# Two crowded experts of a 32-expert loop are moved from loop places 13 and 19 to 11 and 21

## The chip, the cores and the metric
The program runs on one core of one Trainium2 chip. The metric is the time of one execution on the device in microseconds (us); the median of several runs is quoted. "The profiled execution" is one further run whose every instruction was recorded.

## The reference
A sequence of 256 tokens with 1024 features passes through two transformer-like blocks in float32. The first block is a gated recurrence with stick-breaking attention and a convolutional feed-forward part. The second has two kinds of attention and ends in a mixture of experts, which is the part that matters here:

```python
logits = (xf @ w_router + b_router)              # 256 tokens, 32 experts
top_val, top_idx = lax.top_k(logits, 4)          # each token goes to 4 experts
gates = jax.nn.softmax(top_val, axis=-1)
# for every expert e, with the tokens that chose it:
hid = xb @ w_mlp1[e] + b_mlp1[e]                 # 1024 -> 2048
glu = jnp.minimum(hid[..., ::2], 7.0)
lin = jnp.clip(hid[..., 1::2], -7.0, 7.0)
act = glu * jax.nn.sigmoid(1.702 * glu) * (lin + 1.0)
y = act @ w_mlp2[e] + b_mlp2[e]                  # 1024 -> 1024
# out[token] = sum over its experts of gate * y
```

The 256 tokens make 1024 assignments, 32 an expert on average. Every expert's weights, 8 MB and 4 MB, are read from the device's memory once. The order in which the experts are worked through does not change what is computed, apart from rounding.

## The kernel before
The first 740 us or so compute everything up to the router. Then a loop over 32 places begins, one expert at a place. All weights pass through a ring of 17 slots in on-chip memory (`RING = 17`), each slot of 1 MB. An expert takes 12 pieces: 8 of the first matrix ("up") and 4 of the second ("down"). The pieces are loaded and used in a fixed order: up(0), then for each x up(x+1) and down(x). So the first piece of up(x) is number 12x - 4 (`up_at`, line 395), and the last one of all is number 383.

The order of loads is the SyncE queue's (`sync_program`, lines 456 to 466). For piece i it waits until piece i - 17 has been used, and only then issues the load:

```python
e.wait_ge(S.m_piece, i - RING + 1)        # TensorE has used piece i - 17
second, value = K.second_use(i - RING)
e.wait_ge(second, value)                  # line 460: ... and used it a second time, if the expert is crowded
```

A loop place handles a block of up to 64 tokens (`CAP = 64`). On TensorE it is: `up_bias` and 64 matmuls of `up` (line 961), the gather of the next expert's tokens (888), the four down pieces of the expert before (994), transposes (899, 904, 894), and on every second x, `add_pair` (1032), which adds two experts' results to the output. An expert with more than 64 tokens is "crowded": a second block of tokens goes through the same weights while they are still in the ring. `second_block` gathers it, `second_up` (983) does 64 more matmuls, `second_down` (the same line 994, and 1013) 32 more and the sum. Its slots come free only after that second use.

Which expert stands at which place is decided while the kernel runs. `ranks` on VectorE (line 2123) gives each expert a key, its token count times 32 plus a tie value, and its rank is the number of experts with a larger key. Experts 0 and 1 have a large tie value, so they have ranks 0 and 1 and stand at places 0 and 1 always, since their loads start before the routing is known. For the others the host prepares `at`, the rank that is wanted at each place (line 2407), from the list `PLACES`: the most crowded expert goes to the first place of the list, the next to the second, and so on.

```python
at = np.argsort(PLACES)                   # line 2407, host
ts_(K.sel96, at, K.rk[:, 1:2], None, ALU.is_equal)   # ranks(): place of each expert
```

All instructions are in the order in which the program's text puts them on each engine; nothing is reordered by a planner. The list `PLACES` is a constant at the top of the file, so no function's text changes. A program prints what it can find of the functions here:

Of the kernel before, what the change touches and what calls it, by code (L numbers as in the profile page):

```python
# [23 lines left out]
SCN = 14344  # L24


PLACES = [13, 19, 7, 25, 16, 10, 22, 4, 28]
PLACES = [0, 1] + PLACES + [n for n in range(2, NE) if n not in PLACES]


# [2318 lines left out]
def lay_out(i):  # L2349
# [56 lines left out]
    tie = np.where(e < 2, 2.0 ** (20 - e), 1.0 * e)  # L2406
    at = np.argsort(PLACES)
    o["rankc"] = np.concatenate([rep, np.ones((96, 1)) * tie, np.ones((96, 1)) * at], 1).astype(np.float32)
# [21 lines left out]
```

## Time and profile before

| | |
|---|---|
| median of 3 runs | 1726.02 us (1725.83 to 1738.32) |
| profiled execution | 1724.05 us, span of its instructions 1722.3 us |
| TensorE matmuls | 1612.9 us busy, 94% of the span |
| TensorE weight loads | 896.4 us |
| VectorE | 584.1 us |
| ScalarE | 350.6 us |
| bytes moved | 545.47 MB, mean 317 GB/s |

The span runs from the first to the last recorded instruction. Busy shares are averages over parts of the program with different limits, and a matmul that runs counts as busy whether or not the memory would have been the limit at that point; so the loop has to be read stretch by stretch. All times in the rows below are microseconds from the start of the span unless they are marked ns.

### The profile page before, as it was taken

Reading aid. Unit: us, or ns where it says so; the run is one execution under the profiler, and the core shown is the slowest. Engines: PE = TensorE matmul, PEld = TensorE weight load, DVE = VectorE, ACT = ScalarE, POOL = GpSimd, SP = SyncE. Lnnn points to the kernel's source line nnn. Section 1 sums busy time; section 2 is a strip of 40 time slices with the busy share of each in tenths; the row PEclk is TensorE's granted clock in tenths of the full one; section 3 lists DMA queues with packets and bytes.
Section 4 is the critical chain, followed back from the end, with each engine's and each line's share of the span. In section 5 each row is a group of like instructions: output and inputs, shape, how many; then the busy total and the mean of one; then the engine's idle time right before and its main releaser. Section 6 shows DMA issues by size and latency. Waiting matters only on the chain. (4 is left out here: it accounts for less than half of the span.)

```text
span 1722.3 us, 20673 instructions
## 1 busy us (share of the span) xinstructions
PE 1612.9 (94%) x7402; PEld 896.4 (52%) x7402; DVE 584.1 (34%) x1338; ACT 350.6 (20%) x651; POOL 0.2 (0%) x4
## 2 busy tenths in 40 slices
PE   5999989899999898889999998899999999999997
PEld 3888878788888776633333322233333333333222
DVE  2547762789710454331221111111112112211112
ACT  2125562332200134120111101101111011111111
POOL 0000000000000000000000000000000000000000
PEclk9999999999999988988999999999999999999999
DMA  9936665458963330248999999999999999999995
GB/s 397 385 125 254 244 269 184 160 200 325 389 243 125 123 122 1 98 156 357 420 420 419 421 420 421 420 420 421 418 421 385 364 387 420 420 421 420 420 420 235
DMA packets 77220, 545.47 MB, mean 317 GB/s; under 512 B 8944, under 2 KB 9456, under 8 KB 11536
## 3 DMA queue, kind: packets, MB, share of 16 engines
q1 hardware_dynamic: 76048, 542.31, 78.0%
q8 instruction: 93, 1.52, 0.4%
q10 hardware_dynamic: 1024, 1.18, 0.2%
q14 instruction: 55, 0.45, 0.1%
HBM read 542.41 MB, written 1.05 MB: 316 GB/s over the span
## 5 line engine op out<-in xcount | busy, mean ns | idle before, releaser
L961 PE MATMUL bank<-ring,scr 128*64 128x512 f32 x2048 | 456.0, 598 | 18.3 <-DMA ring<-in_w_mlp 18.3
L510 PE MATMUL bank<-hT,ring 128*128 128x256 f32 x1728 | 384.9, 384 | 10.3 <-ACT hT L1141 7.2
L510 PEld LDWEIGHTS bank<-hT,ring 128*128 128x128 f32 x1728 | 332.5, 193 | 60.7 <-issue 15.1
L961 PEld LDWEIGHTS bank<-ring,scr 128*64 128x64 f32 x2048 | 143.2, 138 | 313.5 <-issue 256.6
L994 PE MATMUL bank<-ring,hT 128*64 128x512 f32 x1024 | 233.9, 597 | 2.5 <-DMA ring<-in_w_mlp 2.5
L2215 DVE TENSOR_SCALAR scr<-bank 128x256 f32<-128x256 f32 x64 | 27.0, 421 | 395.5 <-PE bank L961 395.5
L994 PEld LDWEIGHTS bank<-ring,hT 128*64 128x64 f32 x1024 | 68.4, 136 | 141.3 <-issue 130.5
L2285 DVE COPY hT<-bank 64x512 f32<-64x512 f32 x32 | 22.2, 695 | 315.4 <-PE bank L994 285.9
L1452 ACT ACTIVATE scr<-scr 128x256 f32<-128x256 f32 x64 | 26.7, 417 | 503.2 <-DVE scr L2215 503.2
L1569 DVE SCALAR_TENSOR_TENSOR ring<-ring,cb 128x1024 f32<-128x1024 f32 x80 | 94.5, 1219 | 0.0
L674 PE MATMUL bank<-scr,ring 128*128 128x256 f32 x384 | 83.5, 379 | 1.6 <-ACT scr L1295 1.6
L674 PEld LDWEIGHTS bank<-scr,ring 128*128 128x128 f32 x384 | 72.9, 190 | 11.9 <-ACT scr L1295 2.0
L888 PE MATMUL bank<-scr 128*64 128x512 f32 x272 | 69.9, 639 | 7.2 <-DVE scr L2185 4.6
L1486 ACT ACTIVATE hT<-bank 128x512 f32<-128x512 f32 x32 | 19.1, 598 | 221.7 <-PE bank L904 221.7
L1032 PE MATMUL bank<-hT,scr 128*128 128x512 f32 x128 | 59.2, 605 | 0.8 <-ACT hT L1502 0.8
L888 PEld LDWEIGHTS bank<-scr 128*64 128x64 f32 x272 | 20.0, 146 | 47.8 <-issue 39.3
L1032 PEld LDWEIGHTS bank<-hT,scr 128*128 128x128 f32 x128 | 23.0, 189 | 37.6 <-issue 35.9
L904 PEld LDWEIGHTS bank<-con,scr 128*128 128x128 f32 x136 | 14.9, 146 | 35.2 <-issue 26.7
L2173 DVE COPY scr<-bank 64x256 f32<-64x256 f32 x64 | 27.1, 423 | 13.1 <-PE bank L894 11.8
L1634 DVE RECIPROCAL scr<-scr 128x512 f32<-128x512 f32 x8 | 26.8, 3352 | 10.3 <-ACT scr L1172 10.3
L1888 DVE SCALAR_TENSOR_TENSOR scr<-scr,col 128x256 f32<-128x256 f32 x48 | 23.1, 481 | 20.4 <-ACT scr L1295 20.1
L1928 DVE SCALAR_TENSOR_TENSOR xT<-bank,modc,xT 128x256 f32<-128x256 f32 x8 | 3.5, 479 | 77.4 <-PE bank L674 77.4
(389 smaller groups left out, 1350.2 us busy)
## 6 DMA issues: line engine op xcount, KB each, us to landing
ring<-in_w_mlp SPq DMA_DIRECT2D x384, 1024.0 KB, 23.1
ring<-in_w_in SPq DMA_DIRECT2D x28, 1024.0 KB, 24.4
ring<-in_up SPq DMA_DIRECT2D x24, 1024.0 KB, 6.8
ring<-in_w_ada SPq DMA_DIRECT2D x24, 1024.0 KB, 7.0
ring<-in_ada_w SPq DMA_DIRECT2D x16, 1024.0 KB, 5.0
ring<-in_down SPq DMA_DIRECT2D x12, 1024.0 KB, 15.4
ring<-in_ada SPq DMA_DIRECT2D x8, 1024.0 KB, 14.8
ring<-in_w2in SPq DMA_DIRECT2D x6, 1024.0 KB, 9.7
```

The source lines that it names most:

```text
L510: ins = mm(b[:, 256 * j:256 * j + 256], v[:, k * 256 + j * 128:k * 256 + j * 128 + 128], rhs[:, k, :], start=(k == 0), stop=(k == 7))
L674: ins = mm(b[j][:, 0:256], v[:, k * 256 + j * 128:k * 256 + j * 128 + 128], K.ff[:, kk * 8 + k, :], start=(kk == 0 and k == 0), stop=(kk = ...
L888: ins = mm(B[3][64 * hf:64 * hf + 64, :], K.sel[c][:, tt, :], K.h4[:, tt, hf * 512:(hf + 1) * 512], start=(tt == 0), stop=(tt == 1), skip_ ...
L961: ins = mm(HID[0][n][64 * hf:64 * hf + 64, :], K.xe[0][x % 2][:, xo:xo + 64], v[:, o0:o0 + 512], start=False, stop=(k == 7), skip_group_ch ...
L994: ins = mm((K.down_bank(x), B[1])[c][g:g + 64, :], K.aT[c][x % 2][:, 128 * q + 64 * hf:128 * q + 64 * hf + 64], v[:, j * 1024 + oh * 512:j ...
L1032: ins = mm(OUT[tt][oh][:, :], K.pairT[p % 2][oh][:, tt * 128:(tt + 1) * 128], K.ypair[oh], start=False, stop=False, skip_group_check=True)
L1452: act(K.w2[:, sl], K.actb[0][:, sl], ACT.Sigmoid, scale=1.702).then_inc(S.m_sig, 1)
L1569: ins = stt(w, w, 1.0, K.cb[:, :], ALU.mult, ALU.mult, accum_out=K.modc[:, n // 3, m:m + 1])
L1634: e.reciprocal(rst, rst).then_inc(S.vec, done.one())
L1888: stt(w[:, m, :], u[:, m, 1:257], C("fw", 48 + n), w[:, m, :], ALU.mult, ALU.add).then_inc(S.vec, done.one())
L2173: ins = e.tensor_copy(K.pairT[x // 2 % 2][g ^ x % 2][rows, :], B[3][rows, 0:256])
L2215: ts_(w[:, sl], gate, 7.0, None, ALU.min).then_inc(S.m_glu, 1)
```

## The change
The list of wanted places is another one. Places 0 and 1, the completion of the list by the places that it leaves out, and everything else are as before.

```diff
-PLACES = [13, 19, 7, 25, 16, 10, 22, 4, 28]
+PLACES = [11, 21, 27, 6, 16, 8, 24, 13, 18]
 PLACES = [0, 1] + PLACES + [n for n in range(2, NE) if n not in PLACES]
```

The most crowded expert among 2 to 31 moves from place 13 to 11, the next from 19 to 21, the third from 7 to 27, the fourth from 25 to 6, and so on. The number of instructions in the program's text does not change.

## Rows read from the trace of the kernel before

**Rows 1.** The page, 40 slices of 43 us: rate of all transfers.

```profile
GB/s 397 385 125 254 244 269 184 160 200 325 389 243 125 123 122 1 98 156 357 420 420 419 421 420 421 420 420 421 418 421 385 364 387 420 420 421 420 420 420 235
```

**Rows 2.** Windows: length, busy of PE, PEld, DVE, ACT, POOL; clock, DMA share, GB/s.

```profile
1050.00:1100.00 50.00, 44.92 (x198) 13.79 (x196) 7.88 (x22) 4.21 (x9) 0.00 (x0) 1.00 1.01 420
1320.00:1420.00 100.00, 95.94 (x434) 32.92 (x432) 16.81 (x46) 9.56 (x19) 0.00 (x0) 0.98 0.91 367
1430.00:1500.00 70.00, 70.00 (x330) 24.25 (x328) 13.87 (x38) 8.24 (x17) 0.00 (x0) 1.00 1.01 420
```

**Rows 3.** TensorE's timeline, starts of up groups: start, length, [idle before <- releaser].

```profile
1085.88 8.75 PE L961 MATMUL bank<-ring,scr 128*64 128x512 f32 x40
...
1133.79 13.90 PE L983 MATMUL bank<-ring,scr 128*64 128x512 f32 x64
...
1230.07 13.90 PE L961 MATMUL bank<-ring,scr 128*64 128x512 f32 x64
...
1254.48 13.90 PE L961 MATMUL bank<-ring,scr 128*64 128x512 f32 x64
...
1282.68 13.90 PE L961 MATMUL bank<-ring,scr 128*64 128x512 f32 x64
...
1329.52 13.90 PE L983 MATMUL bank<-ring,scr 128*64 128x512 f32 x64
...
1425.41 13.90 PE L961 MATMUL bank<-ring,scr 128*64 128x512 f32 x64
```

**Rows 4.** Groups of instructions: line, shapes, count, busy us, mean ns, idle before.

```profile
L983 PE MATMUL bank<-ring,scr 128*64 128x512 f32 x128 | 27.8, 592 | 0.0
```

**Rows 5.** TensorE's timeline, four pieces that were used as they landed.

```profile
979.19 1.94 PE L961 MATMUL bank<-ring,scr 128*64 128x512 f32 x8 [0.47 <-DMA ring<-in_w_mlp]
...
1099.87 1.94 PE L961 MATMUL bank<-ring,scr 128*64 128x512 f32 x8 [0.55 <-DMA ring<-in_w_mlp]
...
1615.21 1.94 PE L961 MATMUL bank<-ring,scr 128*64 128x512 f32 x8 [0.53 <-DMA ring<-in_w_mlp]
...
1703.44 1.94 PE L994 MATMUL bank<-ring,hT 128*64 128x512 f32 x8 [0.52 <-DMA ring<-in_w_mlp]
```

**Rows 6.** Line 462, one load each (pieces 140, 188): issue, then landing.

```profile
L462 SPq DMA_DIRECT2D ring<-in_w_mlp x1: 5789/5789/5789, 1052.6 to 1052.6; - x1
DMA to landing us min/median/max: 29.5/29.5/29.5
...
L462 SPq DMA_DIRECT2D ring<-in_w_mlp x1: 333/333/333, 1182.0 to 1182.0; - x1
DMA to landing us min/median/max: 20.3/20.3/20.3
```

**Rows 7.** The same for pieces 240 and 272.

```profile
L462 SPq DMA_DIRECT2D ring<-in_w_mlp x1: 1632/1632/1632, 1306.5 to 1306.5; - x1
DMA to landing us min/median/max: 26.8/26.8/26.8
...
L462 SPq DMA_DIRECT2D ring<-in_w_mlp x1: 337/337/337, 1411.3 to 1411.3; - x1
DMA to landing us min/median/max: 13.5/13.5/13.5
```

**Rows 8.** Line 462, loads issued between 1142 and 1210 us.

```profile
DMA to landing us min/median/max: 11.2/15.3/24.6
```

**Rows 9.** Line 462, loads issued between 1306.5 and 1411.6 us.

```profile
DMA to landing us min/median/max: 4.6/8.7/26.8
```

**Rows 10.** SyncE's waits, 1300 to 1430 us: total, times, longest.

```profile
SPq L460 <- PE bank L983: 31.0, 8, 23.3
```

**Rows 11.** The chain of waits that ended last: start, length, link.

```profile
1677.00 26.39 DMA ring<-in_w_mlp
```

## The prediction
> **What bounds the kernel now.** I read the rate of transfers first, over the whole span [rows 1]. In the expert loop, from about 775 us on, it stands at 420 GB/s in almost every slice: the loop is bound by the loading of the weights. Three slices fall below, 385, 364 and 387, between 1292 and 1421 us; there something else was the limit. The windows confirm both: 420 GB/s in 1050 to 1100 us, where TensorE is busy 44.92 of 50 us and so has time to spare, 367 in 1320 to 1420 us, 420 again from 1430 us [rows 2].
>
> What happened in between is seen on TensorE and in SyncE's queue. The second block's matmuls, 128 in all, are exactly two groups of 64, at 1133.79 and 1329.52 us [rows 3, 4]. So two experts are crowded, and they stand at places 13 and 19, as the list says. Around the second one SyncE waits up to 23.3 us for that line before it may issue the next load [rows 10], and the loads of that stretch land 4.6 us after issue at the least [rows 9]: the queue had run dry and each load found idle transfer engines. Around the first crowded expert the fastest landing took 11.2 us [rows 8]: loads still queued, and no slice falls. At the end the last link of the chain is a load again, and the last piece is used as it lands [rows 5, 11]. Hence a transfer time lost anywhere in the loop stands whole in the end, and what follows the last landing (1703.4 to 1722.3 us, 18.9 us) is not touched.
>
> **The pace of both sides.** Landings: piece 99 is used at 979.19 us (the last of up(8)) and piece 147 at 1099.87 us (the last of up(12)), both as they landed: 120.68 / 48 = 2.514 us a piece, 30.17 us an expert of 12. From piece 348 to 383, at the end, it is 88.23 / 35 = 2.521 us [rows 5]. TensorE, when it never waits: up(16) to up(17) 24.41 us, up(17) to up(18) 28.20 us (with the pair's sum), 52.61 us for two, 26.3 us an expert [rows 3]. So TensorE makes up 60.34 - 52.61 = 7.73 us in two experts. A crowded expert costs it: up(18) to up(22) took 142.73 us in place of 105.22, that is 37.5 us more, or 9.7 experts' worth of catching up [rows 3].
>
> **How far TensorE is behind.** I take as lag the start of up(x) less the landing of its first piece. At up(12) it is 1085.88 - (1052.6 + 29.5) = 3.8 us. At up(16), past the first crowded expert, 1230.07 - (1182.0 + 20.3) = 27.8 us [rows 3, 6]. By up(18) it has come down by 7.7 to 20.1 us, and there the second one begins, with 16.3 us more lag than the first had. The ring covers the first one's case and not this.
>
> **The loss, by three counts.** Piece 240 landed at 1306.5 + 26.8 = 1333.3 us, piece 272 at 1411.3 + 13.5 = 1424.8 us [rows 7]: 91.5 us for 32 pieces, 80.4 at 2.514, so **11.1 us** lost. From piece 147 to 348 it is 515.34 us for 201 pieces; at 2.514 they take 505.3, at 2.521 506.7: 10.0 or 8.6 lost [rows 5]. By the rate, (1 - 367/420) of 100 us is 12.6 us [rows 2]. I take 11, because its two landings lie closest around the stall, and keep 8.6 and 12.6 as ends. Since 16.3 us of additional lag cost 11, some 5.3 us of it were still covered.
>
> **The change, part by part.** Nothing is removed or added: as many matmuls, loads, waits and branches, the same work on VectorE in the ranking, with another constant. What moves is this.
>
> (a) The first crowded expert, from 13 to 11. Its additional work begins at the end of place 10. TensorE has caught up with the landings in up(8), at 979 us [rows 5], so it meets place 11 as it met place 13, pinned to the landings; 11 is odd as 13 is, so the pair's sum falls the same way. Its cost to the transfers is that of before, nothing: the cover is the ring, 11.2 us of queue at the narrowest [rows 8]. If that were gone, the cost would be the idle transfer time, at most the 11 us seen at place 19. The lag at up(14) is then the 27.8 us that up(16) had.
>
> (b) The second, from 19 to 21. From up(14) to up(20) are three pairs: 27.8 - 3 x 7.73 = 4.6 us. Within up(20) TensorE takes 13.90 / 8 = 1.74 us a piece against 2.51, so it waits for the eighth if the lag at its start is below 7 x 0.78 = 5.4 us. It is: TensorE is pinned again, as at up(12) with 3.8. And were it 4.6 in full, it is 0.8 above 3.8, under the 5.3 that is covered. The loss of 11 us goes.
>
> (c) The end. Lag at up(24) 27.8 us, at up(30) 4.6, so at up(31) it has caught up. From up(31) to the use of piece 383, 15 landings take 37.7 us, TensorE's work 13.9 + 7 x 1.74 + 3.8 (the pair) = 29.9; another 7.8 us of lag would not show at all.
>
> (d) The uncrowded experts, third rank and below, change places. None has a second block [rows 4], each has the same 12 loads and the same matmuls. An unseen cost is that of other addresses in another order; from both sides, the difference between the two measured paces, 0.007 us x 383 = 2.7 us, more or less. I take none, for both paces were measured across many different experts.
>
> **The sum.** 1724.05 - 11 = 1713.0 us for the profiled execution. It stands 1.97 us under the median of 1726.02, so the median becomes **1715.0 us**, 0.64% less. 1% is 17.3 us, about what a measurement of this kernel can tell from no change.
>
> **A rule that speaks against it.** Spacing matters only because loading leaves TensorE little to catch up with. To work off 37.5 us in six experts it needs 6.25 an expert, so loads that take 26.3 + 6.25 = 32.6 us an expert or more, 12.58 MB in 32.6 us or 387 GB/s and less. Below that rate six places apart are as good as ten, and the time stays at 1726 us. The rows show 420 GB/s in both calm windows [rows 2]. The Trainium skill, "DMA: Bandwidth & Descriptors", section "Specifications", gives about 358 GB/s as the limit of memory for one core, which is below that point; its section "Bandwidth" says that both cores of a pair must be streaming for it. The trace does not agree with the plain limit, by 62 GB/s, so the case gets 1 of 100.
>
> **The rivals.**
> - *Only the place of the stall moves* (6%). The second crowded expert still finds too much lag at up(20), or the first at 11, and part of the transfers' idle time remains. Each us of lag beyond 3.8 + 5.3 = 9.1 at up(20) costs one. If TensorE made up 5 us a pair in place of 7.7, the lag were 12.8 and 3.7 us of the 11 stayed: 1719. Against it stands 52.61 us for two, on the trace without a wait.
> - *Nothing comes of it* (4%, with the 1% of the slower rate). Loading is not what the end waits for: 1726. Against it, the last piece used as it landed [rows 5].
> - *A late end, slower than before* (3%). After place 21 only ten experts are left to catch up in. If TensorE made up d us an expert, the end came 27.8 - 7d - 7.8 us late against the landings. From d = 1.3 down that is more than the 11 won; at d = 0 (15% slower an expert, as if the granted clock fell at times after the second crowded expert) it is 20 - 11 = 9 us slower, 1735. The trace has d = 3.86, and the clock at 1.00 from 1430 to 1500 us [rows 2]; nothing speaks for it.
> - *The change does not do what it says*: the crowded ones aren't ranks 2 and 3, or land at other places. The groups at places 13 and 19 exclude the first [rows 3]; 1%, at 1726.
>
> **How the numbers follow.** The forecast has 86%. Its own range is 1726 less 12.6 and less 8.6, 1713.4 to 1717.4, plus the 2.7 us of (d) either way: 1710.7 to 1720.1. That holds also the first rival's usual case; what is left out (no effect, late end, a small part for surprises) is some 15%. Faster by over 1% (below 1708.8) needs half as much again as was lost: 4%. Slower by over 1% (above 1743.3): 2%; the late end as priced doesn't reach it. Within 1%: 94%.
>
> **What would show it.** Right: no slice of the loop below 415 GB/s until the last; the second-block groups near 1133.8 - 60.3 = 1073.5 and, ten experts of 30.17 us later, 1375 us; landings after both no faster than about 11 us; up(20) with short waits for loads; the last piece about 1692.4 us. The steps fail one by one: (a) if the rate falls near 1130 us, (b) if it falls near 1400 us, (c) if the last pieces are used long after landing, (d) if the pace in calm stretches isn't 2.51 us a piece. The whole would be wrong if the rate is level throughout and the time still stays.

## The result and the profile after

| | before | after |
|---|---|---|
| median | 1726.02 us (20 runs) | 1715.91 us (20 runs) |
| profiled execution, span | 1722.3 us | 1713.9 us |
| ratio of times | | 0.9936, 95% interval 0.9919 to 0.9953 |

The forecast was 1715.0 us, in a range of 1710.7 to 1720.1. The kernel became faster by 0.64%. That is less than the 1% which the prediction took as what a measurement can tell from no change, but the interval of the ratio lies clear of one.

The page of the changed kernel, its line of the rate in 40 slices of 42.8 us, stands against [rows 1]:

```profile
GB/s 397 389 115 264 247 270 185 161 201 320 364 255 124 125 146 1 99 106 359 420 420 420 420 420 420 421 415 421 419 420 420 420 420 407 421 420 420 420 421 219
```

The three slices of 385, 364 and 387 are gone. Two shallow ones came, 415 and 407. They stand behind the two crowded experts at their new places; a repeat of this kernel, further down, shows only the second. The windows answer to [rows 2]; the columns are the same:

```profile
1050.00:1100.00 50.00, 42.98 (x188) 15.08 (x187) 9.62 (x28) 5.73 (x11) 0.00 (x0) 0.93 1.01 420
1320.00:1420.00 100.00, 92.15 (x417) 31.30 (x417) 17.60 (x50) 10.52 (x20) 0.00 (x0) 0.97 1.01 420
1430.00:1500.00 70.00, 69.30 (x326) 24.12 (x324) 12.69 (x35) 8.38 (x16) 0.00 (x0) 1.00 1.01 412
```

From 1320 to 1420 us the rate rose from 367 to 420. What is left of a loss, 412 in the last window, is 70 x 8/420 = 1.3 us.

TensorE's timeline, beside [rows 3], shows where the second blocks stand now (line 983) and up(20) ahead of the second of them:

```profile
1060.64 13.90 PE L961 MATMUL bank<-ring,scr 128*64 128x512 f32 x64
1074.81 13.90 PE L983 MATMUL bank<-ring,scr 128*64 128x512 f32 x64
...
1330.16 12.18 PE L961 MATMUL bank<-ring,scr 128*64 128x512 f32 x56
1342.80 1.94 PE L961 MATMUL bank<-ring,scr 128*64 128x512 f32 x8 [0.46 <-DMA ring<-in_w_mlp]
1364.23 13.90 PE L961 MATMUL bank<-ring,scr 128*64 128x512 f32 x64
1378.40 13.90 PE L983 MATMUL bank<-ring,scr 128*64 128x512 f32 x64
```

The line at 1342.80 is the one to see. TensorE waited for the eighth piece of up(20): it had caught up with the loads one piece before the second crowded expert's additional work began. The load of piece 236, the first of up(20), and below it the fastest landing of the loads issued between 1380 and 1460 us, beside [rows 8, 9]:

```profile
L462 SPq DMA_DIRECT2D ring<-in_w_mlp x1: 5074/5074/5074, 1296.1 to 1296.1; - x1
DMA to landing us min/median/max: 28.7/28.7/28.7
...
DMA to landing us min/median/max: 9.6/14.2/23.0
```

So the lag at up(20) is 1330.16 - 1324.8 = 5.4 us, and no load behind the second crowded expert landed sooner than 9.6 us after its issue, where it had been 4.6. SyncE still waits for line 983, but no longer than 10.0 us at a time, in place of 23.3 [rows 10]. The waits of SyncE's queue from 1380 to 1460 us, total, times, longest:

```profile
SPq L460 <- PE bank L983: 17.4, 8, 10.0
```

The end, from the chain of waits, is bound as before [rows 11], 8.4 us earlier:

```profile
1667.89 27.10 DMA ring<-in_w_mlp
1695.03 1.96 PE bank L994 x8
```

In this execution the loop also began later, its first matmul at 757.7 us, against 756.5 before, so the loop itself became 9.6 us shorter. From last landing to end of span it is 18.9 us in both. TensorE's idle time ahead of line 961 that ended with a load fell from 18.3 us to 9.7: most of what was won is time in which TensorE had stood waiting later in the loop, for loads that the full ring had held back. The group as the two pages have it, before and then after: busy time and mean, then idle time and releaser:

```profile
L961 PE MATMUL bank<-ring,scr 128*64 128x512 f32 x2048 | 456.0, 598 | 18.3 <-DMA ring<-in_w_mlp 18.3
```

```profile
L961 PE MATMUL bank<-ring,scr 128*64 128x512 f32 x2048 | 452.8, 597 | 9.7 <-DMA ring<-in_w_mlp 9.7
```

### The profile page after: what moved, and what is told of

Read it like the earlier page. It is cut to its first block and busy times, and to the rows that moved or that the text cites. A ratio compares the mean times of both kernels' runs of the same rounds, so it can differ in the third digit from the quotient of the medians.

```text
span 1713.9 us, 20673 instructions
## 1 busy us (share of the span) xinstructions
PE 1613.9 (94%) x7402; PEld 899.5 (52%) x7402; DVE 584.1 (34%) x1338; ACT 350.4 (20%) x651; POOL 0.2 (0%) x4
## 5 line engine op out<-in xcount | busy, mean ns | idle before, releaser
L904 PE MATMUL bank<-con,scr 128*128 128x128 f32 x136 | 23.7, 300 | 6.7 <-DVE scr L2244 6.7
```

The costliest lines, as they stand in the source:

```text
L904: ins = e.transpose(B[c][:, 128 * q:128 * q + 128], K.actb[c][:, 128 * q:128 * q + 128], ident)
```

## The experiments

The theory under test: transfers stand still only if TensorE is too far behind when a crowded expert's work begins, so the lag at that point sets the loss. The rivals: some place is bad in itself, the order of the uncrowded experts carries part, only the distance between the two counts, or a stall has a fixed price.

Beside the times, one count is made for every trace: from the landing of piece 96 (about 972 us) to that of piece 383, 287 pieces, which at 2.514 us take 721.5 us. What it took beyond that is called lost by landings: 732.2 - 721.5 = 10.7 us before, 722.5 - 721.5 = 1.0 in the changed kernel. This count does not see what happens ahead of piece 96. Its zero is uncertain by about a microsecond, since 2.514 comes from one stretch of one trace; the differences between traces do not depend on that.

### Each crowded expert alone

```diff
-PLACES = [13, 19, 7, 25, 16, 10, 22, 4, 28]
+PLACES = [11, 19, 7, 25, 16, 10, 22, 4, 28]   # first only
+PLACES = [13, 21, 7, 25, 16, 10, 22, 4, 28]   # second only
```

> Only the first crowded expert moves, 13 to 11; the second stays at 19, so they are eight apart. Ring theory (what counts is how far TensorE is behind when the second one begins, with 9.1 us of lag free): lag at up(18) is 27.8 - 2 x 7.73 = 12.3 us, 3.2 us of transfer time lost, 1719 us, ratio to before 0.996; the dip of the rate near 1370 us is a quarter as deep. Rival, that place 19 itself is bad (what follows it is): nothing gained, 1726. Rival, that the order of all experts in memory counts: no forecast, anything between 1716 and 1726 without a dip that fits.

> Only the second crowded expert moves, 19 to 21; the first stays at 13, eight apart again. Ring theory: the same as with 11 and 19, lag at up(20) 12.3 us, 3.2 us lost, 1719 us, ratio 0.996, and the dip near 1430 us. Rival, that place 19 itself is bad: all of the gain, 1716.

Measured: 1719.51 us (ratio 0.995, interval 0.9929 to 0.9971) and 1719.46 us (0.9952, 0.9928 to 0.9977). The two pages' lines of the rate, first 11 and 19, then 13 and 21:

```profile
GB/s 397 387 110 265 249 269 184 160 201 318 366 252 124 126 144 1 98 120 353 420 420 420 420 420 420 421 419 420 420 420 411 404 391 420 420 420 420 420 420 219
```

```profile
GB/s 397 388 116 264 246 269 185 160 201 322 369 250 123 128 139 1 98 128 352 419 421 420 421 420 420 420 420 413 415 420 420 420 398 387 419 420 421 420 420 234
```

The dip is there in both, shallower, and it moves with the second crowded expert. Place 19 and place 21 cost the same when the first stands eight ahead. The lag at up(18) with 11 and 19:

```profile
1277.39 13.90 PE L961 MATMUL bank<-ring,scr 128*64 128x512 f32 x64
```

```profile
L462 SPq DMA_DIRECT2D ring<-in_w_mlp x1: 3132/3132/3132, 1238.9 to 1238.9; - x1
DMA to landing us min/median/max: 27.4/27.4/27.4
```

1277.39 - 1266.3 = 11.1 us, 12.3 expected. With 13 and 21 it was 14.6 at up(20); at up(16) it had already been 30.0, where it was 27.7 in the kernel before, with a granted clock that fell at the first crowded expert (see the last section). Lost by landings: 3.1 and 4.6 us, that is 2.1 and 3.6 more than in the changed kernel, where the sharp limit of 9.1 us asks for 2.0 and 5.5 at these lags.

### The two alone, and the others alone

```diff
-PLACES = [13, 19, 7, 25, 16, 10, 22, 4, 28]
+PLACES = [11, 21, 7, 25, 16, 10, 22, 4, 28]    # the two alone
+PLACES = [13, 19, 27, 6, 16, 8, 24, 11, 21]    # the others alone
```

In the second list the last two, 11 and 21, stand for the 13 and 18 of the changed list, since 13 is taken.

> The crowded experts at 11 and 21, all others in the order of the list of before. Ring theory: the whole gain, 1716 us, ratio 0.994. Rival, that the order of the uncrowded ones carries part: between 1716 and 1726.

> The crowded experts stay at 13 and 19, ranks four and below go where the changed list has them. Ring theory: 1726 us, ratio 1.000, the same dip of about 11 us after 1320 us. Rival, order of the uncrowded ones: under 1724.

Measured: 1715.92 us (0.9928, 0.9902 to 0.9954) for the two alone, the whole gain. For the others alone the ratio is 1.0005, 0.9986 to 1.0025, no difference that the runs can tell. Its median of 1730.7 us stands above that of before, 1726.82 there. Nine of its twelve executions, and 11 of the 31 of before, had a mean granted clock of 0.970 or less; these took 1728.2 us and more, all others 1729.0 and less. The interval leaves room for some 2 us less or 4 more. By landings the two alone lost 1.2 us, as the changed kernel with its other order (1.0), but the others alone lost 15.9 in place of 10.7: the profiled execution, of 1734.98 us, is one of those with the lower clock, and the last section looks at it.

### Nearer together, and where TensorE is behind anyway

```diff
-PLACES = [13, 19, 7, 25, 16, 10, 22, 4, 28]
+PLACES = [13, 17, 7, 25, 16, 10, 22, 4, 28]   # four apart
+PLACES = [3, 21, 7, 25, 16, 10, 22, 4, 28]    # the first one early
```

> Four apart, 13 and 17. Ring theory: lag at up(16) 27.8 us, 18.7 beyond the free 9.1: 1716 + 18.7 = 1735 us, ratio to before about 1.0045. Rival, that a dip costs about 11 us once it comes, whatever the distance: 1727.

> The first crowded expert at 3, where TensorE is still behind from the start of the loop (lag 35 us at up(2) in the kernel before), the second at 21. Ring theory: the lag is 35 - 9.1 = 26 us beyond what is free, so about 26 us of transfer time are lost near 830 us, none at 21: 1742 us, ratio to before 1.008 or more. Rival, that only the distance between the two counts (18 here): 1716.

Four apart: 1735.0 us. That it is the 1735 of the forecast is partly luck, for in this comparison the kernel before stood at 1729.83 us, not at 1726; the ratio is 1.0035 (1.0007 to 1.0062), 1.0045 forecast. The trace decides: from piece 96 to 383 it took 741.2 us, 19.7 lost by landings, 18.7 more than in the changed kernel. The forecast had the same 18.7 from a lag of 27.8; at the 29.4 that were measured its rule gives 20.3. A fixed price of about 11 us is out. The page's rate falls to 302, at place 17:

```profile
GB/s 397 381 127 250 243 270 184 159 196 336 391 226 125 122 122 1 100 182 366 421 419 420 420 420 420 421 421 410 421 302 350 416 420 420 420 419 420 420 420 228
```

The lag at up(16), ahead of the second crowded expert, is 29.4 us by the unrounded times:

```profile
1231.64 13.90 PE L961 MATMUL bank<-ring,scr 128*64 128x512 f32 x64
```

```profile
L462 SPq DMA_DIRECT2D ring<-in_w_mlp x1: 333/333/333, 1183.6 to 1183.6; - x1
DMA to landing us min/median/max: 18.7/18.7/18.7
```

The first at 3: 1733.42 us, ratio 1.003 (1.0008 to 1.0051), 18 us above the changed kernel, not the 26 expected. Its rate is down from the 20th slice to the 22nd, and level but for one slice of 412 at place 21:

```profile
GB/s 398 375 127 247 241 273 178 166 185 351 393 209 127 132 99 1 97 131 369 319 364 388 421 419 421 420 420 420 420 420 420 420 421 412 420 420 420 420 420 205
```

So distance alone doesn't count: eighteen apart is worse than six if the first one finds TensorE behind. The number was off since the lag at up(2), 35 us, was read from landings that the ring had already held up: in the kernel before it falls to 22.9 by up(3), 6.5 more than the 5.8 that one such expert gives back. 26 - 6.5 = 19.5 would have been the forecast; that was worked out with the result known. From the landing of piece 20 to that of 383 the trace took 938.2 us, against 919.2 in the changed kernel, 19.0 more. A lag is only to be compared where the loads ran level before it.

### Later, and wider

```diff
-PLACES = [13, 19, 7, 25, 16, 10, 22, 4, 28]
+PLACES = [17, 27, 7, 25, 16, 10, 22, 4, 28]   # late
+PLACES = [11, 23, 7, 25, 16, 10, 22, 4, 28]   # wide
```

> Ten apart, but six places later: 17 and 27. Step (c) of the prediction: no transfer time is lost at either, the last piece lands as in the changed kernel, but TensorE's lag of 27.8 us at up(30) is only 22 at up(31) and the last pieces are used 22 - 7.8 = 14 us after landing: 1730 us, and no DMA at the end of the chain. Rival, that ten apart is all that counts: 1716.

> Twelve apart, 11 and 23. No transfer time lost; lag at up(26) 28 us, at up(31) 28 - 15.5 - 5.8 = 6.7 us against an allowance of 6.8 to 7.8 at the end: 1716 us, at the edge. Rival, that wider is better: under 1714. Rival, that the end is late already: 1720.

> The changed kernel once more, on the same chip as its neighbours: 1716 us, rate level, as the mark for the other two.

Late: 1731.79 us, ratio 1.002 (0.999 to 1.0051). The rate holds, down to 405 at the least behind place 27. Piece 383, the last, was issued at 1679.2 us and landed 16.1 later, at 1695.3, within 0.3 us of the changed kernel's:

```profile
L462 SPq DMA_DIRECT2D ring<-in_w_mlp x1: 333/333/333, 1679.2 to 1679.2; - x1
DMA to landing us min/median/max: 16.1/16.1/16.1
```

The end of its chain holds no load. TensorE works through the last five pieces without a wait, until 1714.8 us; the last takes 1.9 of it and so starts at 1712.9, 17.6 us after it landed:

```profile
1700.15 5.30 PE bank L994 x24
...
1706.04 8.77 PE bank L994 x39
```

This is the rival "a late end" of the prediction, made to happen: hardly any transfer time is lost (0.2 us by landings), and yet all of the gain is gone. Wide: 1717.08 us (0.9929, 0.9892 to 0.9967), beside 1715.41 us (0.9913, 0.9883 to 0.9943) of the changed kernel in the same comparison. The two can't be told apart; the lag at up(31), 7.5 us, is at the edge of what the end allows. The rate of the changed kernel in this repeat:

```profile
GB/s 397 389 111 264 251 270 185 160 202 316 365 257 126 123 147 1 99 109 352 421 420 421 420 420 421 420 421 420 420 421 421 420 414 408 420 420 420 420 421 219
```

Behind place 11 there is no dip now, and no landing faster than 11.4 us after issue (9.7 in the first trace of this kernel). The granted clock from 1095 to 1105 us, just behind the second block, was 0.97 here and 0.83 there. Nor does any slice behind place 11 fall below 419 in the three other traces that have the first crowded expert there and 17 slots. So the slice of 415 belongs to that one execution and not to place 11. The dip behind place 21 came again, 414 and 408, with landings of 9.7 us at the least.

### Fewer slots in the ring

```diff
-RING = 17
+RING = 15
```

> The kernel before with 15 ring slots in place of 17. Ring theory: two slots less are 5.0 us less cover in the loop, so the lag that is free falls from 9.1 to about 4 us; the first crowded expert stays about free, the second loses 20.1 - 4.1 = 16 us in place of 11. Rival, that the transfer engines stall for a reason of their own at that place: the loss stays at 11. The part before the loop may become slower too, so the loss is read from the landings around the dip, and the two kernels with 15 slots are compared with each other.

> The changed kernel with 15 ring slots. Ring theory: the second crowded expert meets a lag of about 4 us, at the edge of what is free, so 0 to 2 us are lost at each of the two; the two kernels with 15 slots differ by about 14 us where those with 17 differ by 10. Rival (a stall that belongs to the place): they differ by 10 as before.

Measured: 1734.19 us with 13 and 19 (ratio to before 1.0029, 1.0002 to 1.0056) and 1725.14 us with 11 and 21 (0.9963, 0.9936 to 0.9991). The medians differ by 9.1 us, the ratios by 0.66% or 11 us, with intervals that don't exclude 14. The traces are sharper: 736.0 and 726.8 us from piece 96 to 383, 14.5 and 5.3 lost by landings, a difference of 9.2, where the kernels with 17 slots differ by 9.7. The rates, 13 and 19 first:

```profile
GB/s 397 333 122 256 243 267 183 179 180 324 389 252 113 122 122 1 100 204 355 420 420 420 421 420 420 421 415 405 420 420 373 363 385 420 420 419 420 421 420 233
```

```profile
GB/s 397 336 125 254 244 268 184 180 180 324 389 255 113 123 122 1 98 157 362 420 420 420 420 420 420 407 393 420 420 420 421 420 415 397 421 420 419 420 421 213
```

With 11 and 21 the dips of 407, 393 and 415, 397 now stand at both crowded experts, where 17 slots showed 415 at most and 407. So the cover is the ring: two slots less, and the places that were nearly free cost. But the forecast of 14 us between the two failed. Two slots less cost the pair at 13 and 19 14.5 - 10.7 = 3.8 us, 5 expected, and the pair at 11 and 21 5.3 - 1.0 = 4.3, where 0 to 2 at each of the two were expected. By the difference alone the rival, a stall that belongs to the place, could not be excluded here; the dips at 11 and 21 and the two runs with one expert moved do that. Why the pair at 13 and 19 lost less than 5 more was not pursued.

## Why the prediction was right

**What bounds the kernel.** Right. Where transfer time was lost in the loop, the end moved; and the last landing to the end of the span is 18.9 us before and after.

**(a) 13 to 11 costs nothing.** Right within 1 us. In the first trace the fastest landing behind it is 9.7 us (11.2 at place 13) and one slice stands at 415; in the repeat they are 11.4 us and 420. The lag at up(14) was 1172.3 - 1142.9 = 29.4 us in the profiled execution and 27.3 in the repeat, 27.8 forecast.

**(b) 19 to 21 gives the loss back.** Right: lag 5.4 us at up(20), 4.6 forecast, and a wait within up(20). The free lag of 9.1 us is the part that was too sharp. The lag when the second one begins, against the time:

| crowded at | lag, us | piece 96 to 383, us | lost, us | median, us | before, same comparison |
|---|---|---|---|---|---|
| 11, 21 | 5.4 (up(20)) | 722.5 | 1.0 | 1715.9 | 1726.0 |
| 11, 19 | 11.1 (up(18)) | 724.6 | 3.1 | 1719.5 | 1726.8 |
| 13, 21 | 14.6 (up(20)) | 726.1 | 4.6 | 1719.5 | 1726.8 |
| 13, 19 | 19.8 (up(18)) | 732.2 | 10.7 | 1726.0 | |
| 13, 17 | 29.4 (up(16)) | 741.2 | 19.7 | 1735.0 | 1729.8 |

The kernel before differs by up to 3.8 us between the comparisons, so the medians of different rows can't be subtracted; the landings can. At the long end each us of lag costs about one: 6.1 us for 5.2 from the third row to the fourth, 9.0 for 9.6 to the fifth. At the short end the loss sets in by degrees: 3.6 us for the 9.2 from the first row to the third. A little of it is still there at 11 and 21. In the repeat of the changed kernel and in the two alone it stands behind place 21 only, and the lag at up(20) was 3.9 and 3.8 us there, about what the first crowded expert met at up(10) (3.3 and 3.8). The lag at that point does not explain this rest, and no run was made to find it.

One reading of the prediction was too wide: "each load found idle transfer engines". In the trace of before four loads behind place 19 landed less than 6 us after issue (4.6, 5.8, 5.2, 5.2), and only one of them was issued after all earlier ones had landed; the one of 4.6 us was issued 1.7 us before the load ahead of it landed.

**(c) The end.** Right, and the late pair measured its allowance: a lag of 24.6 us at up(31) ended 17.6 us late, so 7.0 us are allowed, 7.8 forecast.

**(d) The uncrowded experts.** Nothing that can be told from nothing: the two alone lost 1.2 us by landings, the whole list 1.0.

**The sum.** 11 us forecast; 10.1 by the medians, 9.7 by landings. Between the two profiled executions it is 8.4, as the changed one began its loop 1.2 us later.

**The signs.** Not all came as written. The second-block groups stood at 1074.8 and 1378.4 us, forecast 1073.5 and 1375. One slice stood at 407, where none below 415 was to come; the fastest landings were 9.7 and 9.6 us, where about 11 was given; and the last piece was used at 1695.0 us, not at 1692.4: 1.2 us of that is the later start of the loop, the rest comes of 9.7 us won in place of 11.

**The rule that spoke against it.** At a rate of 387 GB/s or less, six places apart would have been as good as ten. Four, six, eight and ten apart gave four different losses by landings, and the page of every kernel here shows 420 GB/s where loads ran freely. The figure of about 358 GB/s that the Trainium skill gives ("DMA: Bandwidth & Descriptors", section "Specifications") does not hold for this core: 420 was measured. The section "Bandwidth" of the same page of the Trainium skill gives it for the case that both cores of a pair stream; whether the other core was idle is not on record here, only that the program runs on one.

## What to carry to other kernels

Where loads bound a loop and some steps carry additional compute, the loads lose next to nothing (about 1 us here) as long as the compute has caught up before the next such step; so measure by how much a plain step catches up (3.9 us here), divide a heavy step's additional time by it (37.5 us, ten steps), and space them by that, as far from the start's backlog and from the end as well. Look for the slices in which the rate falls, then for the fastest landing there: a 1 MB load that lands about 5 us after issue had at most one load ahead of it here. Once the rate is level, more spacing gave nothing (11 and 23).

## What the hardware showed besides

**Time goes with the granted clock, in executions of one kernel.** Of the 20 executions of the changed kernel, the 15 with a mean granted clock of 0.970 to 0.977 took 1710.8 to 1717.4 us, the five with 0.961 to 0.964 took 1723.6 to 1727.9. One trace shows where such time can go. The profiled execution of the kernel with the first crowded expert at 3 (1746.02 us, median 1733.42) began its loop at 768.7 us, the repeat of the changed kernel at 758.4. The window 660 to 680 us, ahead of the loop, where nothing differs in the program, first in that kernel, then in the changed kernel's repeat (clock is the third number from the end):

```profile
660.00:680.00 20.00, 20.00 (x72) 14.20 (x70) 7.28 (x18) 6.79 (x26) 0.00 (x0) 0.50 0.00 1
```

```profile
660.00:680.00 20.00, 16.82 (x113) 12.63 (x113) 9.32 (x24) 10.98 (x38) 0.00 (x0) 0.98 0.00 1
```

At the level of 1.2 GHz (0.50) TensorE did 72 matmuls there without a wait, in place of 113 at 2.4 GHz with short waits between them. Two instructions that both traces have, of lines 761 and 792, stand at 653.75 and 679.41 us in the one and at 656.04 and 672.61 in the other, so 9.1 us went there. Why the clock fell at about 656 us is open: in the 10 us before, at 1.00, TensorE was busy 8.15 us; in the repeat it was busy 7.30 of the 10 us from 650 on, also at 1.00, and the clock held. The executions of the changed kernel near 1727 us would fit the same cause, but none of those was profiled.

**A fallen clock beside a ring that ran dry, and beside one that did not.** With the others moved alone, crowded at 13 and 19, TensorE's clock fell in the gaps of the second crowded expert's gather:

```profile
1310.00:1325.00 15.00, 11.34 (x38) 3.65 (x36) 3.73 (x12) 2.22 (x4) 0.00 (x0) 0.66 1.02 422
```

In the profiled execution of before it was 0.93 in the same window. Up(19) took 15.81 us in place of 13.90, and a landing (piece 241) came 5.7 us late that was on time before; in all 15.9 us were lost by landings in place of 10.7. At 13 and 21 the clock fell the same way at the first crowded expert:

```profile
1115.00:1120.00 5.00, 3.69 (x9) 0.92 (x10) 0.56 (x3) 0.60 (x1) 0.00 (x0) 0.66 1.02 424
```

There the rate only went to 413 and 415, and the 2.3 us of lag that were added at up(16) were paid in part at the second crowded expert. No run held the clock up on purpose, so this is read from traces and not shown by an edit.
